# Decoder layer on one Trainium2 core: who accumulates the middle parts' outputs, and where four pairs' halves of the hidden set are split in the down projection

## What is computed

```python
def swiglu(xn, p):
    return (jax.nn.silu(xn @ p['ffn_w_gate']) * (xn @ p['ffn_w_up'])) @ p['ffn_w_down']
...
    f = swiglu(rmsnorm(x, p['norm_ffn_pre']), p)
    x = x + rmsnorm(f, p['norm_ffn_post'])
```

## Time and profile before

| what | value |
|---|---|
| median of three runs | 3064.79 us |
| the profiled execution, its own time | 3061.94 us |
| its span from first to last instruction | 3060.3 us |
| mean granted clock of PE in it | 0.992 of full |
| down projection on PE, steps 0 to 87 | 2554.2 to 3035.9 us of the span, 481.7 us |

### The profile page before, as it was taken

How to read it: one execution, slowest core, us unless ns; L and a number is a source line. 1 busy time by engine, 2 the same in 40 slices (tenths; PEclk the granted TensorE clock), 3 DMA queues, 4 the chain that set the end, 5 groups by cost and what they waited for, 6 DMA issues and landing times.

```text
span 3060.3 us, 60529 instructions
## 1 busy us (share of the span) xinstructions
PE 2961.7 (97%) x23609; PEld 2843.8 (93%) x23609; DVE 2106.1 (69%) x2964; ACT 1441.3 (47%) x2213; POOL 679.5 (22%) x588
## 2 busy tenths in 40 slices
PE   8999999999999999999997999999999999999999
PEld 6789999998889999987797999999999999999998
DVE  4544337454766487666367899999999997777776
ACT  5442444234365464443356443334433346756666
POOL 0000000001253000000000112222222216688874
PEclk9999999999999999999999999999999999999999
DMA  7553223322216557896765444444444445434434
GB/s 273 186 186 110 82 73 90 96 89 79 77 28 200 167 186 243 275 338 221 255 207 160 121 124 134 127 127 127 125 134 124 123 128 180 140 121 147 157 106 154
DMA packets 457729, 460.61 MB, mean 151 GB/s; under 512 B 22635, under 2 KB 421004, under 8 KB 449695
## 3 DMA queue, kind: packets, MB, share of 16 engines
q1 hardware_dynamic: 436922, 357.88, 37.4%
q0 software_dynamic: 11712, 69.55, 6.0%
q10 hardware_dynamic: 8944, 31.12, 2.8%
HBM read 416.00 MB, written 42.74 MB: 150 GB/s over the span
## 4 chain that ended last, share of the span: by engine, by line
PE 74%; DVE 10%; POOL 5%; issue 4%; ACT 4%; DMA 2%; ACTq 0%; DVEq 0%; SPq 0%; POOLq 0%
PE ps L3238 17%; PE ps L3647 16%; PE ps L3844 10%; PE ps L3846 9%; PE ps L3845 9%; PE ps L3235 5%; POOL down_sums L1042 2%; DVE w_lo L3055 1%; DVE w_low L2077 1%; POOL down_sums L1045 1%; POOL down_sums L1047 1%; ACT w_high L1244 1%; POOL ffn_out L1054 1%; DVE set_low L3071 1%; DMA w_raw<-in_xa_wo 1%
## 5 line engine op out<-in xcount | busy, mean ns | idle before, releaser
L3844 PE MATMUL ps<-set_high,w_hi 128*128 128x260 f32 x3584 | 1016.2, 284 | 30.8 <-DVE prods L2989 14.2
L3846 PE MATMUL ps<-set_high,w_lo 128*128 128x260 f32 x3584 | 1014.2, 283 | 0.0
L3845 PE MATMUL ps<-set_low,w_hi 128*128 128x260 f32 x3584 | 1013.9, 283 | 0.0
L2077 DVE TENSOR_TENSOR w_low<-w_raw,w_high 128x1024 fp32r<-128x1024 f32 x354 | 434.9, 1229 | 622.5 <-ACT w_high L1244 621.9
L3844 PEld LDWEIGHTS ps<-set_high,w_hi 128*128 128x128 f32 x3584 | 676.2, 189 | 36.2 <-DVE prods L2989 16.3
L1244 ACT ACTIVATE w_high<-w_raw 128x1024 fp32r<-128x1024 f32 x356 | 377.1, 1060 | 642.1 <-PE ps L3647 299.4
L3846 PEld LDWEIGHTS ps<-set_high,w_lo 128*128 128x128 f32 x3584 | 677.4, 189 | 0.0
L3845 PEld LDWEIGHTS ps<-set_low,w_hi 128*128 128x128 f32 x3584 | 675.9, 189 | 0.0
L1808 ACT ACTIVATE w_hi<-raw 128x768 fp32r<-128x768 f32 x168 | 142.3, 847 | 467.0 <-PE ps L3846 467.0
L3238 PE MATMUL ps<-x_high,w_high 128*128 128x260 f32 x1568 | 318.7, 285 | 2.7 <-DVE w_low L2077 2.5
L3238 PE MATMUL ps<-x_low,w_high 128*128 128x260 f32 x1568 | 314.4, 282 | 0.0
(11 more groups left out here) (562 smaller groups left out, 5390.6 us busy)
## 6 DMA issues: line engine op xcount, KB each, us to landing
w_raw<-in_w_in SPq DMA_DIRECT2D x96, 512.0 KB
raw<-in_ffn_w_up SPq DMA_DIRECT2D x176, 256.0 KB, 2.9
raw<-in_ffn_w_gate SPq DMA_DIRECT2D x176, 256.0 KB, 3.2
raw<-in_ffn_w_down SPq DMA_DIRECT2D x176, 256.0 KB, 3.1
w_raw<-in_w_out SPq DMA_DIRECT2D x64, 512.0 KB
w_raw<-in_xa_wq SPq DMA_DIRECT2D x64, 512.0 KB
w_raw<-in_xa_wo SPq DMA_DIRECT2D x64, 512.0 KB
set_raw<-h_mid ACTq DMA_DIRECT2D x22, 910.0 KB, 5.6
```

The lines of the kernel that those rows point to most:

```text
L2077: dve.tensor_tensor(w_low[:, slot], w_raw[:, (g.slab0 + jj) % RAW], w_high[:, slot].bitcast(F32), ALU.subtract).then_inc(sem("w_low_ready" ...
L3844: pe.matmul(ps[:, bank, 0:HALF], high, set_high[:, kp, x], start=s + half == 0, stop=False)
L3845: pe.matmul(ps[:, bank, 0:HALF], high, set_low[:, kp, x], start=False, stop=False)
L3846: ins = pe.matmul(ps[:, bank, 0:HALF], low, set_high[:, kp, x], start=False, stop=s == len(tiles) - 1 and half == 1)
```

## The change

Two things are done. First, `add_out` for the units of parts 1 and 2 leaves POOL and is done by DVE, right behind that unit's last step's work (in program order: behind `combine` and, where `combine` is early, behind `down_low` and the second pair too). Second, the eight pairs whose slot has long been free (`spare`) are no longer taken at the head of the step: both `set_high_down` on ACT and `set_low_down` on DVE come behind `down_high(n + 2)` and `down_low(n + 2)`. The ten others (`urgent`) stay where they were. As `early` is computed from the urgent pairs alone, it is false now in steps 27, 30, 51 and 54.

```diff
+        def spare(n):
+
+            return [kp for kp in SET_AT.get(n, []) if set_load_at(kp) > slot_free(kp) + 1]
+
+        def urgent(n):
+
+            return [kp for kp in SET_AT.get(n, []) if kp not in spare(n)]
...
-            def add_out(w):
-
-                p, v, _, _ = UNITS[w]
-                f = ffn_out[:, 2 * v:2 * v + 2].rearrange("p c (h t) -> p (c h) t", h=2)
-                pool.wait_ge(sem("combined"), 4 * (FF + w) + 4)
-                pool.tensor_tensor(f, f, prods[:, 0:4], ALU.add).then_inc(sem("out_taken"), 1)
...
-                        if UNITS[w - 1][0] in (1, 2):
-                            add_out(w - 1)
-                        elif UNITS[w - 1][0] == 3:
+                        if UNITS[w - 1][0] == 3:
...
-                    kps = SET_AT.get(n + 1, [])
+                    kps = urgent(n + 1)
                     for kp in kps[:1]:
                         set_high_down(kp)
                     if n == n0 + ns - 1:
@@ -1996,6 +1996,8 @@
                         set_high_down(kp)
                     if n + 2 < END:
                         down_high(n + 2)
+                    for kp in spare(n + 1):
+                        set_high_down(kp)
                     if n == n0 and w and UNITS[w - 1][0] == 0:
                         copy_out(w - 1)
...
-                    kps = SET_AT.get(n + 1, [])
+                    kps = urgent(n + 1)
                     for kp in kps[:1]:
                         set_low_down(kp)
                     early = kps or p == len(PARTS) - 1
@@ -3133,9 +3134,11 @@
                         set_low_down(kp)
                     if n + 2 < END:
                         down_low(n + 2)
+                    for kp in spare(n + 1):
+                        set_low_down(kp)
                     if not early and n == n0 + ns - 1:
                         out(w)
-                    if n == n0 + ns - 1 and w < len(UNITS) - 1 and p == len(PARTS) - 1:
+                    if n == n0 + ns - 1 and w < len(UNITS) - 1 and p:
                         add_out(w)
```

## The result

The changed kernel takes 3068.17 us, the median of twelve runs (3060.8 to 3071.92); the kernel before takes 3063.62 us in twelve runs of the same day (3061.04 to 3066.1). The ratio of the two sets of runs is 1.0018, with a 95% interval of 1.0010 to 1.0026 (the two medians alone would give 1.0015): slower by 0.18%, just inside the 0.2% called no change, though the interval leaves out 1. The profiled execution has a span of 3064.5 us against 3060.3. It took 3066.10 us, 2.1 less than its median; that of the kernel before took 3061.94, 1.7 less than its own.

The account below looks back on a forecast made before the run. PE, busy 97% of the span, was taken as the bound, so only its waits count; -2.8 + 7.6 - 0.4 - 0.5 = +3.9 us on the median 3064.79 gave 3068.7 us, range 3060.5 to 3074.5.

Parts of the forecast that it names:

- Which places count: Down projection: an edit counts only where PE waits, in six stretches 2.1 to 11.6 us over PE's own pace.
- Four waits for `combine`: Pairs of steps 27, 30, 51, 54 now stand ahead of `combine`: PE waits 3.1 us each, 12.4 us lost.
- Falls of the clock: Three of the four new waits for `combine` are followed by PE's clock falling to half: 5.1 us lost.
- What is given back in these stretches: Steps 27 to 31 and 51 to 55: late slabs and old waits go, 5.4 + 4.5 = 9.9 us gained.
- Part 0: Pairs 4 to 7 (steps 4, 6, 8, 10): four units gain 0.7 us each, 2.8 us, bounds 2.0 to 4.4.
- part 0 without waits: Sign of a wrong forecast: PE would not wait in part 0, where 0.3 to 0.9 us was expected.
- the 0.5 and the 0.57: Part 0, per unit: first product starts 0.5 us earlier; L3063's extra 0.57 us beside POOL's sums may go or stay.
- the 0.7 us a unit: Part 0: gain taken for each of four units, from a span of 0.5 to 1.1 us.
- Steps 40 to 43 and 64 to 66: Four pairs in a row, DVE the bound: moving the addition to DVE gains 0.4 us at step 40, 0.5 at 64.
- addition in every unit: Rival, chance 0.12: DVE's addition becomes a wait in ten units of parts 1 and 2, 6.6 us, giving 3075.3 us.

Follow-up runs that it names:

- third experiment: The changed kernel with `combine` ahead of the spare pair on DVE: 3053.31 us, ratio 0.9964.
- first experiment: The kernel before with only the additions of parts 1 and 2 moved to DVE, all pairs staying where they were: 3056.13 us, ratio 0.9978.
- e5_late_addition: The third experiment's kernel with the additions of units 15 and 23 behind the pairs and slab of steps 40 and 64: 3050.05 us, ratio 0.9957.
- e6_high_half_early: e5_late_addition with ACT's `set_high_down` back at the head of the step, in part 0 only: 3048.74 us, ratio 0.9953.

## Why the prediction was right, and where a term was off

The forecast was 3068.7 us in a range of 3060.5 to 3074.5, slower side of "the same"; measured 3068.17. By its steps:

- **Which places count.** Right in the main. Stretches without a wait before have none after (40.30 us for 8 slabs). But steps 0 to 3 and 16 to 19, which the sum leaves out, moved too (+1.2 and +0.7).
- **Four waits for `combine`, 3.1 us each, 12.4 in all.** Right. PE's starts in the changed kernel show 3.14, 3.06, 3.39 and 3.04, 12.6 in all. Two parts of the term were off and made up for each other: ACT had the high half ready sooner than forecast (DVE's idle time is only 0.80 us), and L3072 took 2.54 us, not the median 2.24; from the last L3056 to `combine` it is 3.94 us, where 1.71 + 2.24 had been put. The third experiment removes the waits by the order alone.
- **Falls of the clock, three of four, 5.1 us.** Mechanism right, number off: behind the waits of steps 28 and 55 the granted clock is 0.50 for 3.41 us, behind those of steps 31 and 52 there is no fall, 3.4 us in all. In the kernel with the pairs alone three of the four are followed by one. No run here varies this by itself, so why one wait is followed by a fall and an equal one isn't stays open. The Trainium skill (TensorE: Matmul & The Clock Gate, "HAM oscillation — how this bites in real kernels") warns of long unbroken idle and would spare waits as short as these; the two falls do not agree with it.
- **What is given back in these stretches, 9.9 us.** Right as a sum: 12.4 + 5.1 - 9.9 = 7.6 was forecast, 2.5 + 3.6 = 6.1 is measured, and the difference is the 1.7 of the third fall, less the 0.2 by which the waits were longer. But the prediction took the old waits as one lot. They hung on one chain, from the addition over the late slab to the late load, and cutting it at either link alone gives about 7 us.
- **Part 0, 2.8 us.** Too small. The same slabs gain 3.8 us in the kernels with the pairs alone and with `combine` first (67.7 to 63.9), inside my 2.0 to 4.4. In the changed kernel it is 6.3, but there the clock was at 0.50 from 2571.03 us, in steps 2 and 3, where the order is still the same; this cost 1.5 us, let the chain catch up, took the 1.3 us wait of step 4 with it and left 0.1 to 0.3 us in steps 6 to 12. The view of PE's waits shows none there at all, and "part 0 without waits" is one of the prediction's own signs of being wrong; with pairs alone or `combine` first, where that fall is missing, waits of 0.7 us stand in steps 6 and 12 and of 0.2 in steps 8 and 10. The mechanism itself came out. From one L2990 to the next it is now 2592.18 to 2602.51 us = 10.33, where it was 11.45 and my lowest was 10.4. The first product's copy starts 6.57 us behind the earlier of the two, where 6.6 was forecast and it was 7.11, and L3064 took 0.95 us and not 1.52. So the 0.5 and the 0.57 of the prediction both came in full in unit 3. What was mis-sized is the 0.7 us a unit taken between them: with `combine` first the four units gain 0.9, 1.1, 1.2 and 0.7. The rows of unit 3 in the changed kernel:

```profile
2592.18 0.69 DVE L2990 TENSOR_TENSOR prods<-ps,prods 128x520 f32<-128x520 f32 x1
...
2597.92 2.51 DVE L3072 TENSOR_TENSOR set_low<-set_raw,set_high 128x1820 fp32r<-128x1820 f32 x1 [0.85 <-ACT set_high L1940]
2600.44 0.69 DVE L3056 TENSOR_TENSOR w_lo<-down_sums,ps 128x512 fp32r<-128x512 f32 x1
2601.05 0.95 DVE L3064 TENSOR_TENSOR w_lo<-raw,w_hi 128x768 fp32r<-128x768 f32 x1
...
2602.51 0.69 DVE L2990 TENSOR_TENSOR prods<-ps,prods 128x520 f32<-128x520 f32 x1
```

```profile
2598.75 0.36 ACT L1868 ACTIVATE prods<-ps 128x260 f32<-128x260 f32 x1
```

- **Steps 40 to 43 and 64 to 66, gains of 0.4 and 0.5.** Wrong in sign by little: +0.5 and +0.1. Slab 41 came 1.6 us earlier as forecast (PE's wait is 1.67 instead of 3.27). Then the two pairs behind the addition took 5.66 us, where they had taken 5.09 (the first two rows below; the third is of the kernel before):

```profile
2780.87 1.23 DVE L3086 TENSOR_TENSOR ffn_out<-ffn_out,prods 128x1040 f32<-128x1040 f32 x1
2782.02 5.66 DVE L3072 TENSOR_TENSOR set_low<-set_raw,set_high 128x1820 fp32r<-128x1820 f32 x2
```

```profile
2782.29 5.09 DVE L3071 TENSOR_TENSOR set_low<-set_raw,set_high 128x1820 fp32r<-128x1820 f32 x2
```

  POOL's sums, which the earlier slab 41 released earlier, began ahead of them (2781.09 against 2782.51). The 0.6 us eat the 0.4: slab 42 starts 15.5 us behind slab 40, where it was 15.4. The rest is the clock. Before, it fell behind slab 41 and the wait for slab 42 hid the cost; now it falls behind slab 42, which the prediction had among its bounds. The first experiment, with the same 15.5 us and no fall, has 26.7 us for steps 40 to 43.
- **The rival "addition in every unit".** Refuted by the first experiment. Waits for slabs of 0.66 us stand in three units of part 3 in every kernel here; what causes them was not tested.
- **Not foreseen.** Steps 16 to 19 are 0.7 us longer; in the two kernels that differ from it by one piece, pairs alone and `combine` first, they are 0.5 shorter than before. Those two lack the fall of the clock in steps 2 and 3. The three profiles that have it (the changed kernel and the two experiments with the late additions) wait 1.2 to 1.4 us in step 19 instead of 0.7 to 0.8, so part of what part 0 caught up may be given back there. No run tests this.
- **The number.** That 3068.17 lies 0.5 us from 3068.7 is in part luck. The three runs that the forecast started from lie 1.2 us above the median of twelve, and the medians differ by 4.5 us where 3.9 was forecast. In the one profile the down projection is longer by 2.4 us, made up of errors that cancel: part 0's pairs gave 3.5 more than forecast and the four waits' stretches cost 1.5 less, against 1.5 too little at steps 40 and 64 and 2.2 in steps 0 to 3, 16 to 19 and 67 to 87, for which the sum had no term.

## What to carry to other kernels

Work that can be done at any time should stand behind everything that is waited for in its step, the last such operation of the in-order queue included: here eight pairs were moved behind one urgent thing (the slab), and four of them in front of another (`combine`), and exchanging the two was worth 15 us. It also has to be asked what comes next in the queue: in part 0 "behind `combine`" is "ahead of the next slab", and cost 5 us. Two waits in one stretch may be one cause and its echo; before adding up what each would give, follow the second one back, here over a load that was issued late because its queue was. And where two halves of a change take away the same waits, neither one's value alone tells what they do together (by the medians -8.1 and +1.1 gave +4.5).

## What the runs showed of the hardware

A DVE operation with two inputs in SBUF and a POOL operation hold each other up, in both directions. L3063 takes 0.944 us at least and up to 2.839 beside `add_out`; in step 28 of the kernel before it starts at 2710.73, while `add_out` runs from 2710.30 to 2712.74, and ends 0.82 us behind it, so nearly all of its own time comes after the earlier trace rows. POOL's row:

```profile
2710.30 2.44 POOL L1054 TENSOR_TENSOR ffn_out<-ffn_out,prods 128x1040 f32<-128x1040 f32 x1
```

In the kernel without additions on POOL it is never over 2.007. The other way round, POOL's sum L1045, 0.742 us by its median, takes 2.43 beside the two pairs that DVE has from 2782.29. Moving the addition onto DVE cost next to nothing: DVE's own busy time fell by 14 us although it got 16 operations of 1.23 us more. That much was expected.

Not expected was that waits of PE between 2.3 and 3.7 us are followed by a fall of the granted clock in some cases and not in others of the same length: behind the wait of 3.66 us for slab 42 it falls in the changed kernel, and behind the 3.65 of the first experiment it does not. Such a fall can also be free. The two last kernels with late additions have the same program in steps 40 to 43. The first two lines below are of `e5_late_addition` (the stretch, then PE's start behind its wait in step 43), the last two of `e6_high_half_early`:

```profile
2764.28:2793.21 28.93, 22.44 (x171) 21.83 (x169) 26.11 (x28) 17.73 (x23) 20.29 (x16) 0.94 0.36 127
2787.27 0.39 PE L3850 MATMUL ps<-set_high,w_hi 128*128 128x260 f32 x1 [2.33 <-DVE prods L2990]
```

```profile
2765.08:2792.22 27.14, 22.34 (x170) 21.73 (x169) 24.84 (x27) 17.50 (x23) 19.92 (x15) 0.94 0.38 131
2787.80 0.39 PE L3850 MATMUL ps<-set_high,w_hi 128*128 128x260 f32 x1 [0.65 <-DVE prods L2990]
```

Each has one fall of 3.41 us. In the second it comes from 2779.46, ahead of the wait in step 43, and the wait is shorter by 1.7 us: PE starts 22.7 us into the stretch, no later than the other's 23.0. In the first it comes from 2787.87, behind the wait, and the stretch is 1.8 us longer.
